# Running decay sums loaded by broadcast into four round buffers, and rope queries split one slot ahead, in a hybrid attention and state-space layer

## The reference, cut to what matters

```python
a_cum = jnp.cumsum(A, axis=2)                       # A = dt * a, in chunks of 128 tokens
seg = a_cum[:, :, :, None] - a_cum[:, :, None, :]
decay = jnp.exp(jnp.where(tri, seg, -jnp.inf))
cb = jnp.einsum('bclgn,bcsgn->bclsg', Cc, Bc)
y_diag = jnp.einsum('bclsgr,bcsgrp->bclgrp', cb[..., None] * decay, X)
decay_to_end = jnp.exp(a_cum[:, :, -1:] - a_cum)
states = jnp.einsum('bclgn,bclgr,bclgrp->bcgrpn', Bc, decay_to_end, X)
chunk_decay = jnp.exp(a_cum[:, :, -1])
...
y_off = jnp.einsum('bclgn,bcgrpn,bclgr->bclgrp', Cc, prev, jnp.exp(a_cum))
...
q_rope = apply_rope(q_rope, positions)
q = jnp.concatenate([q_nope, q_rope], axis=-1)
o = causal_block_attention(q, k, v, QK_HEAD_DIM ** -0.5)
```

## Time and profile before

| | |
|---|---|
| median of 3 runs | 969.84 us (969.01 to 974.21) |
| the profiled execution's own time | 973.06 us |
| its span in the profile | 971.3 us, mean granted clock 0.983 |
| PE busy | 919.2 us (95%) |
| PEld / DVE / ACT / POOL busy | 762.0 / 674.3 / 465.9 / 215.9 us |
| chain that ended last | PE 78%, DVE 9%, ACT 5% of the span |
| DMA | 117.80 MB, mean 121 GB/s |

### The profile page before, as it was taken

How to read it: one execution, slowest core, us unless ns; L and a number is a source line. 1 busy time by engine, 2 the same in 40 slices (tenths; PEclk the granted TensorE clock), 3 DMA queues, 4 the chain that set the end, 5 groups by cost and what they waited for, 6 DMA issues and landing times.

```text
span 971.3 us, 13575 instructions
## 1 busy us (share of the span) xinstructions
PE 919.2 (95%) x4801; PEld 762.0 (78%) x4801; DVE 674.3 (69%) x1102; ACT 465.9 (48%) x730; POOL 215.9 (22%) x117
## 2 busy tenths in 40 slices
PE   4999999999899999999899999999999999999993
PEld 3788778888788878888678788888887788888883
DVE  6979699765767676675446766666666658558958
ACT  3652253443444454434647666566655734323422
POOL 1022112220221212212451323313315000002304
PEclk9999999999999999999989999999999999999997
DMA  9973213211132221322550421421422439534602
GB/s 296 304 266 82 65 43 133 62 43 44 44 109 86 95 99 43 108 86 90 160 184 14 141 78 67 141 89 54 141 99 88 174 116 416 194 130 152 224 3 86
DMA packets 105290, 117.80 MB, mean 121 GB/s; under 512 B 10117, under 2 KB 83942, under 8 KB 105254
## 3 DMA queue, kind: packets, MB, share of 16 engines
q1 hardware_dynamic: 104944, 116.76, 36.3%
q10 hardware_dynamic: 310, 0.57, 0.2%
HBM read 85.59 MB, written 27.79 MB: 117 GB/s over the span
## 4 chain that ended last, share of the span: by engine, by line
PE 78%; DVE 9%; ACT 5%; SPq 3%; issue 3%; DMA 1%; POOL 0%; DVEq 0%; ACTq 0%
PE bank L730 16%; PE bank L732 16%; PE bank L731 16%; PE bank L829 14%; PE bank L984 2%; SPq L399 2%; PE bank L969 2%; PE bank L970 2%; PE bank L971 2%; PE bank L972 2%; PE bank L973 2%; PE bank L859 1%; PE bank L900 1%; PE bank L861 1%; DVE dec L1642 1%
## 5 line engine op out<-in xcount | busy, mean ns | idle before, releaser
L642 POOL TENSOR_TENSOR wl<-wraw,wh 128x1024 fp32r<-128x1024 f32 x31 | 75.3, 2430 | 207.1 <-ACT wh L1170 207.1
L730 PE MATMUL bank<-uh,wh 128*128 128x512 f32 x272 | 108.5, 399 | 1.0 <-DVE ul L1495 0.8
L732 PE MATMUL bank<-uh,wl 128*128 128x512 f32 x272 | 106.6, 392 | 0.0
L731 PE MATMUL bank<-ul,wh 128*128 128x512 f32 x272 | 106.6, 392 | 0.0
L829 PE MATMUL bank<-uh,wh 128*128 128x512 f32 x256 | 103.1, 403 | 0.0
L829 PE MATMUL bank<-ul,wh 128*128 128x512 f32 x256 | 100.7, 393 | 0.0
L730 PE MATMUL bank<-owh,mxh 128*128 128x512 f32 x256 | 100.1, 391 | 0.0
L829 PE MATMUL bank<-uh,wl 128*128 128x512 f32 x256 | 100.0, 391 | 0.0
L731 PE MATMUL bank<-owl,mxh 128*128 128x512 f32 x256 | 99.6, 389 | 0.0
L732 PE MATMUL bank<-owh,mxl 128*128 128x512 f32 x256 | 99.6, 389 | 0.0
L1332 ACT ACTIVATE prob<-bank,small 128x1024 f32<-128x1024 f32 (+3 forms) x64 | 47.5, 742 | 48.7 <-DVE small L1749 48.4
(11 more groups left out here) (232 smaller groups left out, 2274.7 us busy)
## 6 DMA issues: line engine op xcount, KB each, us to landing
wraw<-in_w_in SPq DMA_DIRECT2D x33, 512.0 KB, 3.7
owr<-in_w_out SPq DMA_DIRECT2D x32, 512.0 KB, 4.4
wada<-in_w_ada SPq DMA_DIRECT2D x16, 512.0 KB, 6.0
proj_scratch<-ost SPq DMA_DIRECT2D x16, 512.0 KB, 2.8
xin<-in_x SPq DMA_DIRECT2D x8, 512.0 KB, 6.0
cx<-in_w_ada SPq DMA_DIRECT2D x1, 4096.0 KB, 16.9
ssm_scratch<-xd SPq DMA_DIRECT2D x8, 512.0 KB, 3.5
zs<-proj_scratch SPq DMA_DIRECT2D x8, 512.0 KB, 4.6
```

The lines of the kernel that those rows point to most:

```text
L642: pool.tensor_tensor(wl[:, p], wraw[:, p], wh[:, p].bitcast(F32), ALU.subtract).then_inc(w_split, 1)
L730: pe.matmul(dst, ah, bh, start=start, stop=False)
L731: pe.matmul(dst, ah, bl, start=False, stop=False)
L732: return pe.matmul(dst, al, bh, start=False, stop=stop)
```

## The change

Four edits.

1. The matmuls that spread the sums (`acum_rows`), their selector and the block buffer `bd` go, and with them the doubled scan and the split of the sums. Instead SP stores the 16 rows of sums to four DRAM scratch tensors, and loads four rows at a time, broadcast to all 128 partitions, into `dec`, which now has four buffers, one for each round. `load_acum(r, c)` for a later chunk waits until PE has used the buffer (`y_ready`). ACT's and DVE's operations of a round read `dec` in SBUF in place of the PSUM bank. The mask step now writes over what it reads, so the two reads for `cdv` go ahead of it, with a wait in between.
2. PE's filling is regrouped: five pieces before the transposes in chunk 0 (two in the others), then 4 and 3 (6 and 4) before the two pairs. That is the same number ahead of each remaining step as before.
3. `qr_high` moves from slot 2 to slot 3 on ACT and `qr_low` from slot 1 to slot 2 on DVE.
4. The large buffers' region starts at a multiple of 512. By the sizes in the source it began at byte 23,552 = 46 x 512 already, and begins there now. In the region behind, `exa`, `cts`, `state`, `xd` and others move by some kilobytes; `dec` now starts at 204,736, which is no multiple of 512.

```diff
+        sca = [nc.dram_tensor(f"acum_scratch{r}", [CHUNKS, 4, P], F32).ap() for r in range(4)]
...
-        reg_a, reg_b = end_c, end_c + 52 * 1024
+        reg_a = -(-end_c // 512) * 512
+        reg_b = reg_a + 52 * 1024
...
+            def load_acum(r, c):
+                src = sca[r][bass.ds(address(c), 1)].rearrange("a h l -> (a h) l").partition_broadcast(P)
+                if not isinstance(c, int) or c > 0:
+                    sp.wait_ge(y_ready, 4 * c + r - 3)
+                sp.dma_start(dec[:, r, :].rearrange("p (h l) -> p h l", h=4), src).then_inc(acb_in[r], 16)
...
+            sp.wait_ge(dt_done, CHUNKS)
+            for r in range(4):
+                sp.dma_start(sca[r].rearrange("c h l -> h c l"),
+                             cx[AC0 + 4 * r:AC0 + 4 * r + 4, 12, :].rearrange("h (c l) -> h c l", l=P)).then_inc(acum_out, 16)
             sp.wait_ge(lat_ready, LAT)
             sp.dma_start(scr[0:5].rearrange("t p s -> p t s"), qk[:]).then_inc(y_out, 16)
+            sp.wait_ge(acum_out, 64)
+            for r in range(4):
+                load_acum(r, 0)
...
                 load_tile(1, W_ZSSM + (i + 1) * P, 2 * i + 20)
+                for r in range(2):
+                    load_acum(r, i + 1)
                 store_z(4 * i + 38, 0, i + Z_ATT0)
+                for r in range(2, 4):
+                    load_acum(r, i + 1)
                 store_z(4 * i + 40, 1, i + Z_SSM0)
                 store_y(i)
...
                 fill(fills[1])
-                acum_rows(0, c)
+                y_pair(0, c)
                 fill(fills[2])
-                acum_rows(1, c)
-                fill(fills[3])
-                y_pair(0, c)
-                acum_rows(2, c)
-                fill(fills[4])
-                acum_rows(3, c)
-                fill(fills[5])
                 y_pair(2, c)
...
             def exp_rows(r, c):
-                act.wait_ge(acb_ready, 4 * c + r + 1)
-                act.activation(exa[:, r % 2, :], bk(4 + r % 2), ACT.Exp).then_inc(exa_ready, 1)
+                act.wait_ge(acb_in[r], 16 * c + 16)
+                act.activation(exa[:, r % 2, :], dec[:, r, :], ACT.Exp).then_inc(exa_ready, 1)
...
-                    if i == 3 and more:
-                        weights_high(2 * h + 4, V_W if odd else ROPE_W, after + (2 if odd else 4))
+                    if i == 3:
+                        if more:
+                            weights_high(2 * h + 4, V_W if odd else ROPE_W, after + (2 if odd else 4))
+                        qr_high(not odd, h + 1)
                     if i == 2:
                         probs(0, b, h)
-                        qr_high(not odd, h + 1)
...
                 dve.wait_ge(exa_ready, 4 * c + r + 1)
+                dve.tensor_tensor(cdv[:, 1, 4 * r:4 * r + 4], dec[:, r, P - 1:HB:P],
+                                  bdt[:, AC0 - DT0 + 4 * r:AC0 - DT0 + 4 * r + 4], ALU.subtract).then_inc(rest_ready, 1)
+                dve.tensor_copy(cdv[:, 0, 4 * r:4 * r + 4], exa[:, r % 2, P - 1:HB:P])
+                dve.wait_ge(rest_ready, 4 * c + r + 1)
...
-                dve.wait_ge(stage_ready, c + 1)
-                dve.tensor_copy(bd[0:32, 0, :], stg[0:32, 12, :])
-                dve.tensor_copy(bd[32:64, 1, :], stg[0:32, 12, :]).then_inc(bd_ready, 1)
...
                     if i == 2:
                         inverse_sum(0, h)
-                    if i == 1:
                         qr_low(not odd, h + 1)
```

More of the change, by code:

```diff
@@ L132, in build_layer @@
         ropex, ropes, turns, dtv, sqs, dtw = cx[:, 8, :], cx[:, 9, :], xr[:, 0, 0:S], cx[:, 11, :], cx[:, 10, :], rb[:, 1, :]
-        ach = nc.alloc_sbuf_tensor_at("ach", [P, S], F32R, offset=reg_a + 10 * S * 4)
         (wrx, whx, wlx), e = at(reg_a + 8 * S * 4, [("wrx", [P, KT, P], F32), ("whx", [P, KT, P], F32R), ("wlx", [P, KT, P], F32R)])
         assert e <= reg_a + 11 * S * 4
-        (stg, bd, xdt, bdt, cbs, dec, exa, cts, state, xd, cdv, xdte), e = at(b1, [
-            ("stg", [P, 13, P], F32), ("bd", [P, 2, P], F32R), ("xdt", [P, D], F32), ("bdt", [P, B0 + 2 * P], F32),
-            ("cbs", [P, 2 * P], F32), ("dec", [P, 2, HB], F32), ("exa", [P, 2, HB], F32),
-            ("cts", [P, 2, HB], F32), ("state", [P, D], F32), ("xd", [P, NST, P], F32), ("cdv", [P, 3, SSM_H], F32),
-            ("xdte", [P, D], F32)])
+        (stg, xdt, bdt, cbs, exa, cts, state, xd, cdv, dec, xdte), e = at(b1, [
+            ("stg", [P, 13, P], F32), ("xdt", [P, D], F32), ("bdt", [P, B0 + 2 * P], F32),
+            ("cbs", [P, 2 * P], F32), ("exa", [P, 2, HB], F32), ("cts", [P, 2, HB], F32), ("state", [P, D], F32),
+            ("xd", [P, NST, P], F32), ("cdv", [P, 3, SSM_H], F32), ("dec", [P, 4, HB], F32), ("xdte", [P, D], F32)])
+        assert e - (D + 4 * HB) * 4 >= b1 + (LAT * S + 2 * (S + 4)) * 4
         xdte_at = e - D * 4
@@ L254, in build_layer @@
         xdt_ready = sem("xdt_ready")
-        acb_ready = sem("acb_ready")
+        acum_out = sem("acum_out")
+        rest_ready = sem("rest_ready")
+        acb_in = [sem(f"acb_in{r}") for r in range(4)]
         exa_ready = sem("exa_ready")
@@ L832, in proj_part @@
                     mm.then_inc(proj_ready, 1)
-            def acum_rows(r, c):
-                if r == 0:
-                    pe.wait_ge(bd_ready, c + 1)
-                    pe.wait_ge(xdt_ready, c + 1)
-                if r >= 2:
-                    pe.wait_ge(arg_ready, 4 * c + r - 1)
-                for i in range(2):
-                    j = 2 * r + i
-                    mm = pe.matmul(bk(4 + r % 2)[:, 2 * i * P:2 * (i + 1) * P], selc[:, j:j + 1].to_broadcast([P, P]),
-                                   bd[:].rearrange("p q l -> p (q l)"), start=True, stop=True)
-                mm.then_inc(acb_ready, 1)
             def y_pair(r0, c):
@@ L858, in y_pair @@
                         for q in range(2):
-                            pe.matmul(d[q], xdt[:, own[q]], dec[:, r % 2, of[q]], start=True, stop=False)
+                            pe.matmul(d[q], xdt[:, own[q]], dec[:, r, of[q]], start=True, stop=False)
                         for q in range(2):
@@ L902, in chunk @@
                 mm.then_inc(st_ready, 1)
-            chunk(0, (5, 1, 1, 2, 2, 1))
+            chunk(0, (5, 4, 3))
             with pe.Fori(1, CHUNKS - 1) as c:
-                chunk(c, (2, 2, 1, 3, 2, 2))
-            chunk(CHUNKS - 1, (2, 2, 1, 3, 2, 2))
+                chunk(c, (2, 6, 4))
+            chunk(CHUNKS - 1, (2, 6, 4))
             pe.wait_ge(lat_split, QLT)
@@ L1244, in exp_rows @@
             def exp_rows(r, c):
-                act.wait_ge(acb_ready, 4 * c + r + 1)
-                act.activation(exa[:, r % 2, :], bk(4 + r % 2), ACT.Exp).then_inc(exa_ready, 1)
+                act.wait_ge(acb_in[r], 16 * c + 16)
+                act.activation(exa[:, r % 2, :], dec[:, r, :], ACT.Exp).then_inc(exa_ready, 1)
             def exp_decay(r, c):
                 act.wait_ge(arg_ready, 4 * c + r + 1)
-                act.activation(dec[:, r % 2, :], dec[:, r % 2, :], ACT.Exp).then_inc(dec_ready, 1)
+                act.activation(dec[:, r, :], dec[:, r, :], ACT.Exp).then_inc(dec_ready, 1)
             def chunk(c, more):
@@ L1633, in _ @@
             dve.wait_ge(silu_done, CONVT)
-            dve.memset(bd[:].bitcast(F32), 0.0)
             dve.memset(state[:], 0.0).then_inc(state_new, 1)
@@ L1652, in ssd_round @@
                 dve.wait_ge(dec_ready, 4 * c + r + 1)
-                de = dec[:, r % 2, :].rearrange("p (h l) -> p h l", h=4)
+                de = dec[:, r, :].rearrange("p (h l) -> p h l", h=4)
                 dve.tensor_tensor(de, de, cbs[:, g * P:(g + 1) * P].unsqueeze(1).to_broadcast([P, 4, P]),
@@ L1951, in constants @@
     t[:, 0], t[:, 1], t[:, 2], t[:, 3] = np.tile(inv, 4), phase, phase / (2 * np.pi), RMS_EPS
-    t[0:16, R_HI], t[16:32, R_HI], t[16:32, R_LO] = 1.0, -1.0, 1.0
-    for j in range(8):
-        for block in range(2):
-            head = 2 * j + block
-            t[[32 * block + head, 32 * block + 16 + head], R_SEL + j] = 1.0
     return t
```

36 lines of the change are left out of this document (14 added, 22 removed).

## The result

The changed kernel takes 949.17 us in the median (947.13 to 951.49, four executions), the kernel before in the same sitting 969.42 (968.48 to 974.21). By the medians that is 20.25 us less; the measured ratio, with its 95% interval, is 0.9777 [0.9756, 0.9798]. The prediction said 949.6 in 943.5 to 958.0.

A forecast was written before the change was run, and what follows sets the result against it. PE was taken to bound the chunk loop, with further losses in waits and slow clock between heads. Chunk stage 7.4 plus heads 12.8 gave 20.2 us off the median 969.84: 949.6 us, range 943.5 to 958.0.

The forecast's parts named there:

- Spreading matmuls, 1.06 a chunk: Chunks 1 to 6: removing four matmul pairs a chunk gains 1.06 us each, 6.4 us over six periods.
- Chunk 0, 0.3: Chunk 0, not PE-bound: earlier rounds against POOL's split on round 2, 0.3 us gained out of 0 to 1.06.
- DVE's margin, 1.6 us: Chunk loop: DVE's round 3 ends at T + 20.4, 1.6 us before PE comes to the second pair at T + 22.0.
- The loads of the sums, nothing: SP's broadcast loads of the decay sums arrive in time, even at 10 us each; no cost.
- The mask step from PSUM to SBUF, nothing: DVE's mask step in each round: reading SBUF in place of PSUM makes no difference in time.
- The last chunk, 0.7: Last chunk: 0.7 us gained, between -0.5 and 1.5; PE's wait of 1.89 and the slow clock behind it stay.
- The gaps of the heads, 8.2: Between heads: moving the rope step a slot earlier removes PE's waits for rope queries, 8.2 us over heads 0 to 6.
- The clock, 3 x 1.54: Heads begun after gaps of 1.75 us lose their slow clock: 1.54 us each for three heads, 4.6 us.
- Head 6: End of head 6: POOL's last gate operation holds DVE's rope step, so only 0.5 of 1.75 us is gained.
- The 512 rounding, nothing: Start of the large buffers: rounding to a multiple of 512 moves nothing, by the addresses; no gain.
- the chunk stage's 7.4: Whole chunk stage: 6.4 for chunks 1 to 6, 0.3 for chunk 0, 0.7 for the last chunk, 7.4 us gained.
- the heads' 12.8: All heads: 8.2 us of gaps plus 4.6 us of slow clock, 12.8 us gained.

The follow-up runs named there:

- sums_only: The changed kernel with the rope step back at its old place (third edit undone); 963.63 us against 970.84 for the kernel before, ratio 0.9926.
- late6: The changed kernel with DVE's product of C and the exps made six times more in round 3 of every chunk; 979.75 us.
- before480: The kernel before with its large buffers starting 32 bytes lower, 480 above a multiple of 512; 978.73 us against 970.82.
- rope_only: The kernel before with the moved rope step (third edit) alone; 956.78 us against 970.84, ratio 0.9865.
- late2: The changed kernel with DVE's product of C and the exps made two times more in round 3 of every chunk; 956.3 us.

## Why the prediction was right, point by point

- **Spreading matmuls, 1.06 a chunk:** right to the hundredth, 6.36 for six periods. Differences of start times, not durations, gave it.
- **Chunk 0, 0.3:** 0.27. Its last wait grew from 0.63 to 1.23 while the matmuls went, as two things running against each other.
- **DVE's margin, 1.6 us:** right in kind, about 0.7 short. I reckoned against the pair's start at T + 22.0; but PE needs round 3's product only for the pair's second half, 0.92 later (353.25). I had also said that POOL's splits spare the rounds, and they don't: the first small operation of a round has two SBUF inputs. In round 0 it took 1.68, since the split ends at T + 5.4, behind a skip product that waits for a store (5.4 us to landing, 3.5 before); that fits into DVE's wait for PE behind round 1 and cost nothing. In round 2, which began at T + 15.3, it took 0.5 beside the second split, and round 3 ended at T + 21.0 instead of T + 20.4. The reading of the earlier trace rows was off too: POOL's operation there ends 2.36 after DVE's starts, not 2.15, which leaves 1.1 and not 1.3; the conclusion, that DVE waits, stands.
- **The loads of the sums, nothing:** right, 3.7 us each, and no wait on PE for them; DVE's only wait of this kind in chunk 1 is 0.17 for `exa` in round 2, for ACT.
- **The mask step from PSUM to SBUF, nothing:** right. Before and after, the groups of all such steps:

```profile
L1642 DVE SCALAR_TENSOR_TENSOR dec<-bank,bdt,mask_ls 128x128 f32<-128x128 f32 x128 | 36.0, 344 | 39.3 <-ACT exa L1246 39.3
```

```profile
L1639 DVE SCALAR_TENSOR_TENSOR dec<-dec,bdt,mask_ls 128x128 f32<-128x128 f32 x128 | 36.5, 347 | 0.0
```

  344 and 347 ns. By the table of the Trainium skill, "VectorE: DVE Perf Modes", section "The TRN2 errata — SBUF-src ops pay a fixed extra latency per instruction", it would have been 62 cycles, by an estimate 65 ns, less. No run here shows such a difference.
- **The last chunk, 0.7:** mis-sized. The profiled pair gives 3.83, but that trace is the one in which the clock stayed at 1.00. `sums_only`, whose clock fell, took 45.49 against 46.99: 1.5. Over seven traces with the changed last chunk the mean is 44.9 (43.2 to 46.2), over three with the old one 46.5 (46.0 to 47.0): 1.6, and the two ranges overlap a little. What failed here is the claim that the slow stretch stays: it stayed in six of the seven, for 3.4 to 10.2 us, and not in the profiled one.
- **The gaps of the heads, 8.2:** the gaps were read right (8.1 went), their cost was not. Over a whole head the interval shrank by the gap and 0.23 to 0.33 more in each of the seven (in heads 3 and 5 beyond the clock's 1.5 as well): 1.9 us that the sum didn't have. They are of two kinds. PE and ACT at the end of head 2 before, where the first scores of head 3 follow at 606.74, then PE after:

```profile
604.22 0.39 PE L732 MATMUL bank<-qlh,hwl 128*128 128x512 f32 x1
604.66 0.32 PE L984 MATMUL bank<-ident,prob 128*128 128x128 f32 x1
...
604.13 0.40 ACT L1340 ACTIVATE prob<-prob,small 128x128 f32<-128x128 f32 x1
```

```profile
589.84 0.40 PE L753 MATMUL bank<-qlh,hwl 128*128 128x512 f32 x1
590.08 0.28 PE L985 MATMUL bank<-ident,prob 128*128 128x128 f32 x1
590.32 0.49 PE L970 MATMUL bank<-knh,qnh 128*128 128x512 f32 x1
```

  From the last transposes to the scores, start to start, it is 2.08 before and 0.24 after: 1.84 for a gap of 1.75, since a matmul that follows at once starts before the one ahead of it ends. Over the seven heads this gives 0.04 to 0.25 each, 1.1 together. The rest is a second wait that shows no gap in the timeline. The step to the transposes themselves is 0.44 before and 0.24 after. They wait for ACT's normalising, which ended at 604.53, behind the rope copy of 1.06 us; after, it ended 1.2 us ahead of them. This took 0.1 to 0.2 at the end of each even head, 0.8 together; in every trace with the copy at its new place the step there is 0.23 or 0.24. In `late6` too a gap of 1.67 costs 2.0 of period, 1.84 of it at the gap itself and the rest in the few matmuls behind it.
- **The clock, 3 x 1.54:** right for the two traces that were compared: 1.5 and 1.5 in heads 3 and 5, beyond their gaps, and 1.6 behind head 7's scores. But the term was read in an execution 3.6 above the median and then taken from the median. Of the 33 executions of before that ran beside the experiments, one has a mean granted clock of 0.983 like the profiled one, all others 0.986 to 0.990; `sums_only` (0.987) and `before480` (0.985) show two such falls and not three. For the median two are likelier, 3.1 us, an estimate from these clocks.
- **Head 6:** right. The wait went from 1.75 to 1.37, for the reason given (POOL); 0.38 of the 0.5 that I had. In seven other traces with the step at the same place it is 1.15 to 1.70.
- **The 512 rounding, nothing:** right as a difference to before, whose buffers start at 23552, a multiple of 512 as well. But with the selector and its constants gone the small buffers end at 23488, by the sizes in the source, and without the rounding the change would have lost 7.0 of its 20. The edit that I passed over in one sentence is worth as much as the whole chunk stage.

So the sum met the time to 0.4 us with three terms off, and that is luck: the last chunk is worth about 1 more than I had and the heads' gaps 1.9 more, while the clock's term is probably 1.5 too large for a median execution. The mechanisms held. By the medians the chunk stage's 7.4 met 7.2 in `sums_only` and the heads' 12.8 met 14.1 in `rope_only`; the halves together are 1 us more than the whole change, which lies within their intervals and is not resolved.

## What to carry to other kernels

Price a gap from start to start of the matmuls around it, not by its idle time, and a removed matmul in the same way; and look at what the moved operation holds up besides, for a wait of 0.2 us shows no gap. A cost that comes and goes from execution to execution can't be read in one trace and taken from the median. When a small buffer goes away, look at where all later ones start: loads that write 512 bytes per partition lost a sixth of their rate when they began 64 bytes off, and none at 256. A margin measured in a steady loop says nothing about its first and last turn.

## What the runs showed of the hardware that I had not expected

- Loads with 512-byte pieces: 347 GB/s from a start at a multiple of 512 bytes, 343 at 256 above (one of two buffers moved), 290 at 448 or 480 above, 291 at 64 above in a stretch with loads of the moved buffer alone. A load of 512 KB took 6.0 or 7.4 us.
- A DVE operation with two SBUF inputs waited for a POOL operation that was under way, however small it was: four columns took 1.68 us, the rope step 2.62 instead of 1.22, six products 9.57 instead of 4.32. The Trainium skill, "SBUF — State Buffer", section "Who interferes with whom", says that such an instruction contends with a GpSimd one that reads SBUF, and calls the shared ports an exclusive lock; by that rule, the trace agrees.
- The granted clock fell to its lower level (1.2 of 2.4 GHz) behind one of four gaps of 1.65 us and behind nine of twelve of 1.75, with the same work around them, and stayed up behind one of 1.81 in the last chunk. In the last head of `late2` it fell at 755.53, with gaps of only 0.85 and 1.11 just ahead, which left it at 1.00 in the thirteen other traces. From the gap alone it couldn't be foretold here.
